# Spills of x on another queue, an earlier eviction, a fourth staging buffer, and the last pair's weights on one engine, in a two-layer encoder trunk

## The reference, cut to what matters

```python
h = rmsnorm(x, g_mix[i]);  proj = h @ w_in[i]
mixed = short_conv_mixer(...) if i == 0 else stick_breaking_attention(...)   # 16 heads of 64
mem_out = memory_cross_attention(q_mem, rmsnorm(mem, g_mem[i]) @ w_mem_kv[i], g_q[i], g_k[i])
x = x + concatenate([mixed, mem_out]) @ w_out[i]
h = rmsnorm(x, g_ffn[i])
gate, up = split(h @ w_ffn_in[i])          # 2816 columns each
x = x + (silu(gate) * up) @ w_ffn_out[i]
```

## Time and profile before

| what | value |
|---|---|
| median of three runs | 2764.35 us |
| profiled execution, its own time | 2765.97 us |
| span of its profile | 2764.4 us |
| TensorE busy | 96% |
| VectorE, ScalarE, GpSimd busy | 52%, 38%, 18% |
| mean granted TensorE clock | 0.982 of 2.4 GHz |
| chain of waits that ended last | TensorE 77%, VectorE 10% |

### The profile page before, as it was taken

The page is one execution under the profiler, slowest core; times in us unless marked ns, Lnnn a source line. Parts: engine busy times, 40 slices in busy tenths (PEclk is TensorE's granted clock), DMA queues, the critical chain, the costliest instruction groups (busy, mean ns, idle before and its releaser), DMA issues.

```text
span 2764.4 us, 35260 instructions
## 1 busy us (share of the span) xinstructions
PE 2656.8 (96%) x12704; PEld 2209.7 (80%) x12704; DVE 1425.1 (52%) x1773; ACT 1046.6 (38%) x1719; POOL 508.5 (18%) x425
## 2 busy tenths in 40 slices
PE   7999999998999999999999999996999899999999
PEld 7888888886888887888878888885887788887887
DVE  6454445166444442324677777777237544444131
ACT  6450103133333341213666666665233333333020
POOL 2200000102222310021033333331101222321000
PEclk9999999999999999999999999997999999999999
DMA  6401111122223243104111111112212223226111
GB/s 206 145 28 49 46 46 54 46 84 99 88 94 106 87 152 141 53 32 152 47 36 32 32 30 31 30 30 108 99 41 111 97 85 106 89 78 245 42 53 72
DMA packets 57414, 221.44 MB, mean 80 GB/s; under 512 B 7280, under 2 KB 7280, under 8 KB 52080
## 3 DMA queue, kind: packets, MB, share of 16 engines
q1 hardware_dynamic: 43920, 164.68, 17.7%
q0 software_dynamic: 13120, 49.29, 5.1%
q10 hardware_dynamic: 288, 6.29, 0.6%
HBM read 170.43 MB, written 49.81 MB: 80 GB/s over the span
## 4 chain that ended last, share of the span: by engine, by line
PE 77%; DVE 10%; issue 5%; ACT 4%; DMA 2%; POOL 1%; SPq 1%; ACTq 0%; DVEq 0%; POOLq 0%
PE ps L1771 24%; PE ps L1773 24%; PE ps L1772 24%; DVE w_lo L1201 1%; DVE xg_lo L1207 1%; DVE keep L1433 1%; DVE aT_lo L1475 1%; DMA stage<-d_act 1%; DVE tile_lo L1617 1%; PE ps L2067 1%; PE ps L2051 1%; DVE x L1643 1%; POOL sig L657 1%; PE ps L2068 1%; ACT keep L932 1%
## 5 line engine op out<-in xcount | busy, mean ns | idle before, releaser
L1771 PE MATMUL ps<-xg_hi,w_hi 128*128 128x512 f32 x1344 | 537.7, 400 | 7.8 <-DVE xg_lo L1559 4.9
L1773 PE MATMUL ps<-xg_hi,w_lo 128*128 128x512 f32 x1344 | 527.6, 393 | 0.0
L1772 PE MATMUL ps<-xg_lo,w_hi 128*128 128x512 f32 x1344 | 526.7, 392 | 0.0
L1771 PE MATMUL ps<-tile_hi,g_hi 128*128 128x512 f32 x1064 | 419.4, 394 | 23.1 <-ACT gate L1121 23.1
L1773 PE MATMUL ps<-tile_hi,g_lo 128*128 128x512 f32 x1064 | 417.6, 393 | 0.0
L1772 PE MATMUL ps<-tile_lo,g_hi 128*128 128x512 f32 x1064 | 415.5, 391 | 0.0
L1771 PEld LDWEIGHTS ps<-xg_hi,w_hi 128*128 128x128 f32 x1344 | 254.5, 189 | 58.2 <-issue 6.2
L1773 PEld LDWEIGHTS ps<-xg_hi,w_lo 128*128 128x128 f32 x1344 | 254.0, 189 | 55.0
L1772 PEld LDWEIGHTS ps<-xg_lo,w_hi 128*128 128x128 f32 x1344 | 254.8, 190 | 48.5 <-issue 0.7
L1771 PE MATMUL ps<-act_hi,d_hi 128*128 128x512 f32 x704 | 279.0, 396 | 6.4 <-DVE act_lo L1718 6.3
L1773 PE MATMUL ps<-act_hi,d_lo 128*128 128x512 f32 x704 | 277.1, 394 | 0.0
(11 more groups left out here) (212 smaller groups left out, 4031.6 us busy)
## 6 DMA issues: line engine op xcount, KB each, us to landing
raw<-wpack SPq DMA_DIRECT2D x108, 512.0 KB, 3.6
quads<-wpack SPq DMA_DIRECT2D x38, 1024.0 KB, 5.3
d_raw<-wpack SPq DMA_DIRECT2D x32, 704.0 KB, 4.2
stage<-d_act POOLq DMA_DIRECT2D x44, 512.0 KB, 6.8
d_act<-up SPq DMA_DIRECT2D x38, 256.0 KB, 2.1
d_act<-gate SPq DMA_DIRECT2D x38, 256.0 KB, 2.2
d_x<-x SPq DMA_DIRECT2D x16, 512.0 KB, 6.4
x<-d_x SPq DMA_DIRECT2D x16, 512.0 KB, 4.5
```

The lines of the kernel that those rows point to most:

```text
L1771: pe.matmul(out, whi, mhi, start=start, stop=False, skip_group_check=chained)
L1772: pe.matmul(out, whi, mlo, start=False, stop=False, skip_group_check=chained)
L1773: return pe.matmul(out, wlo, mhi, start=False, stop=stop, skip_group_check=chained)
```

## The change

1. The eight spills of `x` in the feed-forward part are issued by GpSimd, each behind the sum of squares of its block, and no longer by SP. In layer 1 the first waits until `x` is back from the attention's spill, which lies in the same tensor.
2. On VectorE, `fill(up, 5)` and `gated(R, 2)` stand ahead of granule 6 and tile 5.
3. `R` is a fourth stage for the first half's activations; the load of activation j waits for the split of j-4. For the second half, the loads of activations 0 to 2 wait for the last reader of their own stage.
4. In the attention's last pair GpSimd multiplies both rows.

```diff
-        stage = [place(f"stage{j}", [P, SEQ], F32, STAGE_AT[j]) for j in range(CHUNK)]
+        stage = [place(f"stage{j}", [P, SEQ], F32, STAGE_AT[j]) for j in range(CHUNK)] + [R]
...
-        STAGED = (5, 5, 4) + (1,) * (CHUNK - 3)
+        STAGED = (4, 4, 4) + (1,) * (CHUNK - 3) + (2,)
...
-            s = j if c else j % 3
-            return s, 16 * (STAGED[s] * (i + 1) if c else STAGED[s] * i + j // 3 + 1)
+            s = j if c else (0, 1, 2, CHUNK)[j % 4]
+            return s, 16 * (STAGED[s] * (i + 1) if c else STAGED[s] * i + j // 4 + 1)
...
-                e0 = base["E", i][2]
-                for m in range(KB):
-                    sp.wait_ge(evacuated, e0 + 2 * m + 2)
-                    sp.dma_start(d_x[:, m, :], x[:, m, :]).then_inc(fx_spilled, 16)
-
...
-                                for r in range(1 if last else 2):
+                                for r in range(2):
                                     weigh(hp * ROWS + (2 * (it + 1) + r), (it + 1) % 2, r, (it + 1) % 4)
...
-                for m in range(KB - 2):
-                    add_squares(2 * i + 1, m)
+                for m in range(KB):
+                    if m < KB - 2:
+                        add_squares(2 * i + 1, m)
+                    pool.wait_ge(evacuated, base["E", i][2] + 2 * m + 2)
+                    if i % 2 == 1 and m == 0:
+                        pool.wait_ge(x_back, 16)
+                    pool.dma_start(d_x[:, m, :], x[:, m, :]).then_inc(fx_spilled, 16)
...
-                            elif j > 2:
-                                pool.wait_ge(act_lo_ready, FBLK * i + j - 2)
+                            elif j > 3:
+                                pool.wait_ge(act_lo_ready, FBLK * i + j - 3)
                         elif j < 3:
-                            pool.wait_ge(act_lo_ready, FBLK * i + (10, 11, 11)[j])
+                            pool.wait_ge(act_lo_ready, FBLK * i + 9 + j)
...
-                                    if last and r == 1:
-                                        dve.wait_ge(scanned, row + 1)
-                                        dve.wait_ge(sig_ready, row + 1)
-                                        own = sig[:, (it + 1) % 2, r, 0:n - 1]
-                                        dve.tensor_tensor(own, own, keep[:, (it + 1) % 2, r, 1:n], ALU.mult
-                                                          ).then_inc(a_ready, 1)
...
-                granule(6, 0, 0)
-                whole_tile(5)
                 dve.wait_ge(act_stored[0], 16 * (STORED[0] * i + 2))
                 fill(up, 5, banks_of[5])
                 gated(R, 2)
+                granule(6, 0, 0)
+                whole_tile(5)
                 whole_tile(6)
```

More of the change, by code:

```diff
@@ L380, in trunk @@
         act_stored = [sem(f"act_stored{h}") for h in range(2)]
-        stage_landed = [sem(f"stage_landed{j}") for j in range(CHUNK)]
+        stage_landed = [sem(f"stage_landed{j}") for j in range(CHUNK + 1)]
         act_hi_ready = sem("act_hi_ready")
@@ L1492, in pair @@
                                 for r in range(2):
-                                    row, n = hp * ROWS + (2 * (it + 1) + r), key_count(r, (it + 1) % 4)
+                                    row = hp * ROWS + (2 * (it + 1) + r)
                                     scan(row, (it + 1) % 2, r, (it + 1) % 4)
```

## The result

The changed kernel takes **2725.44 us** (median of four runs, 2724.61 to 2726.01), the kernel before 2765.42 in the runs beside it (2763.78 to 2768.6): a ratio of 0.9854, 95% interval 0.9837 to 0.9871. The forecast was 2725.0. The profiled execution took 2724.61 us with a span of 2723.0, so 41.4 us of span are gone.

A forecast was written before the change was run, and what follows sets the result against it. TensorE was taken as the bound, busy 96% of the span, so gains were its waits and slow-clock time. Terms 27.1+1.7+7.5+3=39.3 us off 2764.35 gave 2725 us, range 2716 to 2740.

The forecast's parts named there:

- the floor: Feed-forward part: TensorE ends unit 5 near 645.1, so the third block's product cannot end before 647.6.
- Gate and `w_lo`: Feed-forward part: TensorE's two waits for the `gate` copy and slow restarts go, 27.1 us, plus 1.7 for the weight-split wait.
- taken to be as long: Slow matmuls after layer 1's `gate` wait were assumed to lose 2.0 us, as in layer 0.
- layer 1 is taken to be alike: Entry to the down projection: layer 1 was assumed to lose 1.5 us at the lower clock, as layer 0 does.
- The upper end, 9.3: Fourth staging buffer: most it could gain at the down projection's entry, 6.3 us of waits plus 2x1.5 of slow clock.
- The others swap little: Last attention pair: the longest two weights gain about 1.2 us each on GpSimd, the shorter ones change little.
- The bounds of -4 and 10: Last attention pair: range in us for moving VectorE's multiplications to GpSimd, with 3 us taken as the gain.
- The DMA engines set the entry: Rival, chance 0.14: DMA engines, not buffers, bound the down projection's entry; the fourth buffer gives 0, 2732.5 us.
- The wait moves to tiles or quads: Rival, chance 0.08: TensorE's wait moves to tiles 5 and 6 or the second quads, half the gain left, 2739 us.
- Part 4 costs its 3.9: Rival, chance 0.10: GpSimd's multiplications in the last pair lose 3.9 us instead of gaining 3, 2732 to 2734 us.
- Slower, the spills hold up the weights: Rival, chance 0.03: GpSimd's spills delay the out projection's weight loads, costing 55 us, so 2780 us.
- The change moves nothing: Rival, chance 0.03: VectorE's own load fills the time without the spill, buffers and weights cancel, 2764 us.

The follow-up runs named there:

- the table of all kernels: Compares the kernel before, the changed kernel and its edited variants over the last pair plus 32 out-projection steps: 71.7 to 74.9 us.
- longest weights alone: Changed kernel, but in the last pair GpSimd multiplies row 1 only where it has 1024 keys, VectorE the shorter ones: 2725.87 us.
- all eight without them: The changed kernel and seven edited variants with its same instructions in the last pair: 71.7 to 73.1 us for the pair and 32 steps.
- part 1 undone: Changed kernel with the eight spills of x issued by SP again, behind the last weight load: 2747.97 us.

## Why the prediction was right

**Part 1, right by its steps.** VectorE was to start 8.8 us earlier and did by 598.18-589.46=8.7, released by the wait that was named, ScalarE's `R`. With the eight spills undone, 12.15 us of waiting came back and 23.7 us in the two feed-forward stages. Two kernels settle why: the spills on SP at an earlier place do as well, and twice the bytes do no harm. The place in SP's queue was the cause, not the engine, the queue's kind or the bytes.

**Part 2, right in the times, wrong as a part of its own.** The third product was put at 647.6 and ended at 647.48; the splits of tiles 5 and 6 were put at 654 and 656, and both were over at 648.00+6.72=654.7 with no wait behind them. 2.1 us for the meeting with GpSimd's sums were right too: the two tiles ahead of the product took 4.50 us together, the two behind it 6.72, and it is the second of these that starts at 650.20 beside a sum that runs from 650.16 to 652.57 and takes 4.52 instead of 2.28. But the text did not say how little part 2 would be worth alone: the floor (TensorE has to end unit 5 first) leaves 0.8 to 2.4 us of room with it and the old order takes 2.9 of them (the product then starts 59.7 us behind the scaling of x instead of 56.8), so it was worth 1.6 us.

**Gate and `w_lo`: 29.9 us against 27.1+1.7=28.8.** Most of the 1.1 us is known. Layer 1's restart was "taken to be as long" as layer 0's; in the kernel before its twelve steps from 2150.23 to 2155.49 took 5.26 us instead of 2.76, 2.5 us lost and not 2.0. And the shifts at `w_lo` were 1.1 us each instead of the wait's 0.85, another 0.5.

**Part 3: 9.8 us against 7.5, a term mis-sized.** The step that failed is "layer 1 is taken to be alike". In layer 1 of the kernel before the entry has two waits and a longer slow stretch behind the second (12 steps of 0.43 us against layer 0's 5):

```profile
2523.49 0.50 PE L1771 MATMUL ps<-act_hi,d_hi 128*128 128x512 f32 x1 [0.53 <-DVE act_lo L1718]
...
2528.22 0.79 PE L1771 MATMUL ps<-act_hi,d_hi 128*128 128x512 f32 x1 [3.07 <-DVE act_lo L1718]
```

Behind it 14 steps, from 2528.22 to 2534.35, took 6.13 us instead of 3.2, so 2.9 us were lost where 1.5 had been taken: there was 9.3+1.4=10.7 to be had, and of that 9.8 came, with 1.0 us of waits left. The upper end, 9.3, was too low for the same reason. Nor was a fifth lost to the busy DMA engines: the landing of 7.9 us is still long, but in time. Undoing the part gave back 7.7 in the down projections: its two waits are 6.1 us, and layer 1's restart has 7 slow steps instead of 12.

**Part 4: some 2 us against 3, a term mis-sized.** The trace pair of before and after gives 1.6 us, of which only some 0.5 lie in the pair; the table of all kernels gives 2.2, 1.5 at the least. "The others swap little" left out that three of the four scans behind the shorter weights get 0.2 to 0.7 us longer, 1.4 together; how much of this reached TensorE is not shown, since taking those weights back (longest weights alone) moved nothing. Here the rule of the Trainium skill (SBUF — State Buffer, Who interferes with whom), that a VectorE instruction with two SBUF inputs and a GpSimd one that reads SBUF exclude each other, fits the traces: each scan is longer by nearly what is left of the GpSimd weight when it starts (0.67 for 0.80 us, 0.58 for 0.76, 0.24 for 0.37). The prediction worked out 1 us by it from whole weights of 1.1 to 2.0 us; but the scans start late in those weights or after them, so its 1 was no nearer than the 3 of the sum. The bounds of -4 and 10 were never near.

**Why the total is nearer than its terms**: +1.1 and +2.3 against -1.4 leave +2.0 or so, the span's 41.4 against the sum of 39.3; the medians, 2765.42 and 2725.44, differ by 40.0. That the time came out within 0.5 us of 2725 is partly luck: the errors of the terms cancel in part, and the spread of the last pair alone is larger.

**The rivals.** *The DMA engines set the entry*: no, part 3 alone is worth 7. *The wait moves to tiles or quads*: no, the trace lists no wait of TensorE at all from 590 to 740 us. *Part 4 costs its 3.9*: no, both kernels with VectorE's weights are slower in that stretch than all eight without them. *Slower, the spills hold up the weights*: it needed 5.5 us of delay. A weight load that met spills in the changed kernel (DMA issues from 478 to 484 us) took 1.0 us more than the usual 3.6:

```profile
d_x<-x POOLq DMA_DIRECT2D x2, 512.0 KB, 4.1
raw<-wpack SPq DMA_DIRECT2D x1, 512.0 KB, 4.6
```

and doubling the spills moved nothing. The 16.2 us on which this rival stood were also not the 4 MB spill's alone: three of GpSimd's 512 KB loads (`k_lo`, `v_hi`, `v_lo`) were still under way when that weight load was issued, the last landing 7.5 us after. *The change moves nothing*: out by 41 us.

## What to carry to other kernels

Follow a long wait back over the engines to where something was complete and not yet sent: a DMA in the wrong place of an in-order queue can cost 12 us a layer that show up 60 us later under another line's name, and its place matters, not the engine that issues it. Edits on one chain don't add: price them together, since each alone hides behind what the other leaves, and price them in the stages that they touch, since the others move by a microsecond or two by themselves. In a stretch where the matmul engine waits in many short pieces, count what the lower clock costs the others, and try idle matmuls in the waits, but only where the wait is longer than they are.

## What was not expected of the hardware

- The same instructions took 61.5 to 64.2 us in the last pair, though no edit had touched them: 61.5 to 63.0 at a granted clock of 0.85 over 57 us, 63.5 to 64.2 at 0.76. A comparison of two kernels by 2 us in such a stretch says little.
- Added matmuls made the kernel faster: with 48 in the pair and 12 behind it the granted clock went from 0.76 to 1.00, and the pair took 59.0 us instead of 64.2 (some of this may be VectorE's, since these kernels also weight only the longest rows on GpSimd; the idle matmuls without that took 60.5) and the restart behind it 1.5 us less.
- The slow stretch behind a wait has no fixed length: behind the same 3.33 us wait at the out projection it was 6 slow steps in the changed kernel, 10 with the longest weights alone and 13 with part 1 undone. Among the eight kernels with the same pair, those with the lower clock in it had fewer slow steps behind it.
- A VectorE scan that starts beside a GpSimd multiplication is longer by nearly the rest of that multiplication (0.67 for 0.80 us), and not at all if it starts after it (2.02 us).
- A spill of 512 KB took 2.9 us by GpSimd's queue when alone or in pairs, 6.4 us by SP's with eight in a row; the queue had less to do with it than the company, as GpSimd's second copy of a pair took 3.8.
